# A third late tile searched by VectorE beside the attention steps, late gates from tile 21, and scores ahead of values on TensorE

## The reference, cut to what matters

```python
h = rms_norm(x, norm_g); p = h @ w_in                      # 1024 -> 2884 columns
qa, ka, va, ga, qb, kb, vb, gb, qi, ki, wi = split(p)      # ga, gb: gates of the two head groups
oa = sink_attention(window of 128 keys)                    # group A, heads 0..7
r = relu(einsum('qhe,le->qhl', qi, ki))                    # indexer
score = einsum('qhl,qh->ql', r, wi); score = where(adm, score, -inf)
_, idx = top_k(score, 256)                                 # 256 keys for each query
ob = softmax(q kT + bias over idx) v                       # group B, heads 8..15
y = x + concat(oa * silu(ga), ob * silu(gb)) @ w_out
```

## Time and profile before

| | us |
|---|---|
| median of 3 runs | 5192.75 (5189.86 to 5194.4) |
| profiled execution | 5191.41 |
| its span | 5189.6 |
| stage one, stage two, last stage in the span | 2488.8, 2103.4, 597.4 |
| busy: TensorE, its weight loads | 4365.5 (84%), 2717.3 (52%) |
| busy: VectorE, ScalarE, GpSimd | 3466.5 (67%), 3454.7 (67%), 1623.0 (31%) |

### The profile page before, as it was taken

How to read it: one execution, slowest core, us unless ns; L and a number is a source line. 1 busy time by engine, 2 the same in 40 slices (tenths; PEclk the granted TensorE clock), 3 DMA queues, 4 the chain that set the end, 5 groups by cost and what they waited for, 6 DMA issues and landing times. The chain is left out here.

```text
span 5189.6 us, 78325 instructions
## 1 busy us (share of the span) xinstructions
PE 4365.5 (84%) x26505; PEld 2717.3 (52%) x26505; DVE 3466.5 (67%) x6644; ACT 3454.7 (67%) x6887; POOL 1623.0 (31%) x1358
## 2 busy tenths in 40 slices
PE   6767777777687786767689999989999999989999
PEld 3334443434343343433466767767777776754444
DVE  1266788888797898988476766676666668625111
ACT  1578788988787797872478888858787785520100
POOL 1345556667557756777110000000000000000000
PEclk9888888888788898988799999999999999999999
DMA  6211111100010111001521111011010010034423
GB/s 143 66 44 43 37 38 39 34 30 34 30 44 32 37 45 39 33 32 56 157 64 52 43 50 39 27 53 39 25 41 25 27 37 26 12 112 134 112 102 101
DMA packets 201975, 276.98 MB, mean 53 GB/s; under 512 B 50496, under 2 KB 134176, under 8 KB 201056
## 3 DMA queue, kind: packets, MB, share of 16 engines
q1 hardware_dynamic: 198624, 271.81, 16.6%
q10 hardware_dynamic: 2960, 0.17, 0.0%
HBM read 156.73 MB, written 114.16 MB: 52 GB/s over the span
## 5 line engine op out<-in xcount | busy, mean ns | idle before, releaser
L595 PE MATMUL bank<-w,x 128*128 128x512 f32 (+1 forms) x2848 | 1245.9, 593 | 26.3 <-DVE w L940 13.7
L1042 DVE TENSOR_SCALAR_CACHE_REDUCE ties<-score,cand 128x512 int8<-128x512 f32 (+13 forms) x448 | 1110.5, 2479 | 122.3 <-POOL score L916 106.9
L595 PEld LDWEIGHTS bank<-w,x 128*128 128x128 f32 x2848 | 571.3, 204 | 608.2 <-issue 540.1
L806 ACT ACTIVATE act_junk<-score,a_cand,a_sign 128x384 int8<-128x384 f32 (+13 forms) x420 | 879.4, 2094 | 14.0
L1832 DVE CUSTOM_DVE_ANT_0 row<-bank,mask 128x512 f32<-128x512 f32 (+3 forms) x1024 | 622.5, 638 | 384.1 <-PE bank L1571 383.5
L613 PE MATMUL bank<-kiT,qi 128*128 128x512 f32 (+3 forms) x1136 | 394.2, 489 | 414.9 <-DVE kiT L960 211.4
L1538 POOL TENSOR_TENSOR near_bias<-table,mask 128x2048 f32<-128x2048 f32 (+1 forms) x32 | 129.5, 4047 | 1830.6 <-DVE part L1832 1815.1
L1766 ACT ACTIVATE pT<-bank 128x512 f32<-128x512 f32 (+2 forms) x704 | 368.0, 523 | 449.3 <-PE bank L1587 447.3
L1587 PE MATMUL bank<-ident,row 128*128 128x128 f32 x4224 | 607.3, 283 | 52.0 <-DVE pT L1943 43.4
L1668 ACT ACTIVATE row<-row,top 128x1024 f32<-128x1024 f32 (+7 forms) x640 | 632.9, 990 | 3.4 <-DVE top L1845 3.4
L1571 PE MATMUL bank<-kT,qb 64*128 64x256 f32 (+1 forms) x4352 | 608.4, 396 | 7.9 <-DVE part L1832 5.1
(11 more groups left out here) (255 smaller groups left out, 4904.9 us busy)
## 6 DMA issues: line engine op xcount, KB each, us to landing
qk_t<-ring SPq DMA_DIRECT2D x66, 256.0 KB, 2.0
gates<-ring SPq DMA_DIRECT2D x66, 256.0 KB, 2.0
gate<-gates SPq DMA_DIRECT2D x33, 512.0 KB, 3.4
out<-x_in SPq DMA_DIRECT2D x33, 512.0 KB, 2.9
x<-in_x_prompt SPq DMA_DIRECT2D x32, 512.0 KB, 3.8
mixed<-mixT SPq DMA_DIRECT2D x64, 256.0 KB, 2.0
mix_in<-mixed SPq DMA_DIRECT2D x32, 512.0 KB, 4.5
x_in<-in_x_prompt SPq DMA_DIRECT2D x32, 512.0 KB, 3.9
```

The costliest lines, as they stand in the source:

```text
L595: ins = pe.matmul(p_bank[n % 2][:, 0:n1 - n0], held[:, c * P:(c + 1) * P], w[:, c, n0:n1], start=(c == 0), stop=(c == KC - 1))
L806: tick(act.activation(junk, row, ACT.Sign, bias=c, scale=back, accum_out=a_sum[:, :]))
L1042: n = tick(dve.tensor_scalar(ties[:, 0:width], row, c.bitcast(F32), 0.0, ALU.is_ge, ALU.add, accum_out=counts[:, i:i + 1]))
```

## The change

1. `SEARCHED` goes from 30 to 29: tile 29 is no longer searched in stage one; its scores are stored like those of 30 and 31. In stage two ScalarE still searches 30 and 31 in the same tiles. VectorE searches tile 29 by itself (`test_search`), in pieces of 512 scores, with 289 portions laid evenly over the 408 wide steps of tiles 3 to 26, one portion at most between its copy and its use of scores.
2. The closing is rewritten. Tiles 30, 29 and 31 are closed in tiles 19, 27 and 29, in pieces of 512 (`close`); the mask and tie buffers hold a single piece. ScalarE stores each piece to `chosen` at the end of the step after its last portion, and VectorE's next piece waits for that store (`s_lst`). For 30 and 31 the ties are now counted beforehand by a second set of counting passes. A closing of a ScalarE tile has 34 portions, that of tile 29 has 24. SyncE loads late masks from `chosen` as it does the others. A second late row (`test_row`, 1.9 MB) is loaded at the start of stage two.
3. `LATER_FROM` goes from 23 to 21: the late gates of tiles 0 to 9 are projected in steps 21 to 30.
4. In stage two TensorE's step is transposes, scores or gate, values.

```diff
-SEARCHED = TILES - 2
+SEARCHED = TILES - 3
-LATER_FROM = 23
+LATER_FROM = 21
-LATE_SPANS = {1: ((3, 27, 28),), 2: ((3, 18, 19), (20, 28, 29))}[len(LATE_TILES)]
+ACT_TILES = LATE_TILES[1:]
+ACT_SPANS = ((3, 18, 19), (20, 28, 29))
+DVE_TILE = LATE_TILES[0]
+DVE_SPAN = (3, 26, 27)
...
+for _a, (_first, _last, _close) in zip(ACT_TILES, ACT_SPANS):
+    share(LATE_ACT, _first, _last, TESTS * (len(quarters(_a)) + 1) + 1)
+    share(LATE_DVE, _close, _close, 2 + 2 * len(quarters(_a)) + 3 * len(pieces(_a)))
+share(LATE_TEST, *DVE_SPAN[0:2], TESTS * (len(pieces(DVE_TILE)) + 1) + 1)
+share(LATE_DVE, DVE_SPAN[2], DVE_SPAN[2], 3 * len(pieces(DVE_TILE)))
...
 # load_mask
                 if t in LATE_TILES:
-                    sp.wait_ge(s_lmask, LATE_TILES.index(t) + 1)
-                    sp.dma_start(mask[t % 2][:, 0:near], late_mask[:, 0:near]).then_inc(s_m[t % 2], 16)
-                    sp.dma_start(mask[t % 2][:, near:near + NEAR], late_mask[:, near:near + NEAR]).then_inc(s_m[t % 2], 16)
-                    return
+                    sp.wait_ge(s_lst, 16 * STORED[t, len(pieces(t)) - 1])
...
 # TensorE, stage two
                     turn(n, g)
-                    if last is not None:
-                        apply(*last)
-                    last = (n, g)
                     for kind, m, j in PLACED[n, g]:
                         if kind == "score":
                             score(m, j)
                         else:
                             turn_gate(m, j)
+                    if last is not None:
+                        apply(*last)
+                    last = (n, g)
...
 # ScalarE, stage two, at the end of a step
+                    for a, q in STORES[n, g]:
+                        act.wait_ge(s_lmask, PIECE_AT[a, q] + 1)
+                        for c, m, to in stores_of(a)[q]:
+                            act.dma_start(chosen[a, :, to:to + m], late_mask[:, c:c + m]).then_inc(s_lst, 16)
...
 # VectorE, stage two
+            def close(a, held, known):
+                for q, (c, n) in enumerate(pieces(a)):
+                    at, piece, tie = held[:, c:c + n], late_mask[:, 0:n], late_tie[:, 0:n]
+                    if PIECE_AT[a, q]:
+                        dve.wait_ge(s_lst, 16 * list(STORED.values())[PIECE_AT[a, q] - 1])
+                    dve.wait_ge(s_dve, tick.n)
+                    tick(dve.tensor_scalar(piece, at, known, -BIG, ALU.is_le, ALU.mult))
+                    tick(dve.tensor_scalar(tie, at, known, None, ALU.is_equal))
+                    yield
+                    dve.wait_ge(s_dve, tick.n)
+                    tick(dve.tensor_tensor_scan(at, tie, tie, held[:, c - 1:c] if c else 0.0, ALU.add, ALU.max))
+                    yield
+                    dve.wait_ge(s_dve, tick.n)
+                    m = tick(dve.scalar_tensor_tensor(tie, at, left, tie, ALU.is_le, ALU.mult))
+                    dve.wait_ge(s_dve, m)
+                    m = tick(dve.scalar_tensor_tensor(piece, tie, BIG, piece, ALU.mult, ALU.add))
+                    dve.wait_ge(s_dve, m)
+                    dve.nop(nofuse=True).then_inc(s_lmask, 1)
+                    yield
...
+            def test_search():
+                dve.wait_ge(s_trow, 16)
+                m = tick(dve.memset(d_cand[:, 0:1], 0))
+                for i in range(TESTS):
+                    b = 31 - i
+                    c, to = d_cand[:, i % 2:i % 2 + 1], d_cand[:, (i + 1) % 2:(i + 1) % 2 + 1]
+                    for q, (c0, n) in enumerate(pieces(DVE_TILE)):
+                        dve.wait_ge(s_dve, tick.n)
+                        m = tick(dve.tensor_scalar(test_junk[:, 0:n], test_row[:, c0:c0 + n], c.bitcast(F32), 0.0, ALU.is_ge, ALU.add,
+                                                   accum_out=d_part[:, q:q + 1]))
+                        yield
+                    dve.wait_ge(s_dve, m)
+                    m = tick(dve.tensor_reduce(d_counts[:, i:i + 1], d_part[:, :], AX.X, ALU.add))
...
                     dve.tensor_copy(pT[1][at % 2][:, 0:cols], t_bank[1][:, 0:cols]).then_inc(s_c1, 1)
+                    for _ in range(LATE_TEST[n, g]):
+                        next(tests, None)
```

More of the change, by code:

```diff
@@ L1305, in quarters, with pieces, share, stores_of @@
     return [(c, min(QUARTER, (a + 1) * P - c)) for c in range(0, (a + 1) * P, QUARTER)]
+def pieces(a):
+    return [(c, min(STEP, (a + 1) * P - c)) for c in range(0, (a + 1) * P, STEP)]
 LATE_ACT = {_s: 0 for _s in STEP_AT}
 LATE_DVE = {_s: 0 for _s in STEP_AT}
[L1310 to L1316, removed]
+LATE_TEST = {_s: 0 for _s in STEP_AT}
+def share(count, first, last, many):
+    steps = wide_steps(first, last)
+    for i in range(many):
+        count[steps[i * len(steps) // many]] += 1
+for _a, (_first, _last, _close) in zip(ACT_TILES, ACT_SPANS):
[3 more added lines that the diff above has]
+share(LATE_DVE, DVE_SPAN[2], DVE_SPAN[2], 3 * len(pieces(DVE_TILE)))
+def stores_of(a):
+    far, near = ((a - 2) // 4 + 1) * STEP, (a - 1) * P
+    stores = []
+    for c, n in pieces(a):
+        parts = [(c, min(c + n, near) - c, c)] if c < near else []
+        if c + n > near:
+            at = max(c, near)
+            parts.append((at, c + n - at, far + at - near))
+        stores.append([(at - c, m, to) for at, m, to in parts])
+    return stores
+STORED, PIECE_AT = {}, {}
+for _, _a in CLOSED:
+    for _q, _parts in enumerate(stores_of(_a)):
+        PIECE_AT[_a, _q] = len(STORED)
+        STORED[_a, _q] = len(_parts) + max(STORED.values(), default=0)
+STORES = {_s: [] for _s in STEP_AT}
+for _close, _a in CLOSED:
+    _steps = wide_steps(_close, _close)
+    _front = 2 + 2 * len(quarters(_a)) if _a in ACT_TILES else 0
+    _many = _front + 3 * len(pieces(_a))
+    for _q in range(len(pieces(_a))):
+        _last = _steps[(_front + 3 * _q + 2) * len(_steps) // _many]
+        STORES[list(STEP_AT)[STEP_AT[_last] + 1]].append((_a, _q))
 def exps_of_job(n):
@@ L1415, in stage_two @@
         s_lmask = sem("late_mask_ready")
+        s_lst = sem("late_mask_stored")
+        s_trow = sem("test_row_loaded")
         s_lact = sem("late_act_ticks")
@@ L1516, in _ @@
             sp.wait_ge(s_win, 32)
+            sp.wait_ge(s_lst, 16 * max(STORED.values()))
         @block.gpsimd
@@ L1692, in late_search @@
                 act.wait_ge(s_lmade, 1)
-                for i, a in enumerate(LATE_TILES):
+                for i, a in enumerate(ACT_TILES):
                     width, parts = (a + 1) * P, quarters(a)
@@ new lines, in _ @@
+            over, left, value, low, step, more = (l_pick[:, i:i + 1] for i in range(6))
+            def close(a, held, known):
[12 more added lines that the diff above has]
+                    m = tick(dve.scalar_tensor_tensor(tie, at, left, tie, ALU.is_le, ALU.mult))
+                    dve.wait_ge(s_dve, m)
+                    m = tick(dve.scalar_tensor_tensor(piece, tie, BIG, piece, ALU.mult, ALU.add))
+                    dve.wait_ge(s_dve, m)
@@ L1927, in _ @@
+            tests = test_search()
             late_work = late_close()
```

126 lines of the change are left out of this document (70 added, 56 removed).

## The result

The changed kernel takes 5161.0 us (median of four executions, 5160.8 to 5161.1) against 5192.75: 31.8 us or 0.6% faster, the ratio 0.9939 with a 95% interval of 0.9923 to 0.9955. A fifth execution was in a slower state, 5740.5 us at a granted clock of 0.73, and is left out. Forecast were 5196 us, no change, with a range from 5163: the kernel is faster, and just outside the range. The profiled execution took 5160.8 us, its span 5159.0.

A forecast was written before the change was run, and what follows sets the result against it. No engine fills the first stage; TensorE (93% busy) bounds the attention stage. Terms -31 - 4 + 38 + 1 = +4 us on 5191.4 gave 5195.4 in the profiled execution's terms, 5196 beside the median; range 5163 to 5226.

The forecast's parts named there:

- Stage one: First stage without the search of tile 29, early gates included: -31 us, between -12 and -45.
- (b): First stage, score row 31: GpSimd's eight units take 66.4 us against 86.7 without VectorE's scans beside them, -20.3 us.
- the tail: First stage, from row 31's end to the stage's end (25.7 us): fewer late gates and stores in the way, -3.7 us.
- The +3 us for the early gates: First stage: late gates two tiles sooner delay the moment tile 28 is found by 3 us (-5 to +12).
- The closings: Attention stage, closing the three late tiles in tiles 19, 27 and 29: +27, +6 and +5, together +38 us.
- B's sign (under 100): Attention stage: tile 19 under 100 us would show that the closings are cheap.
- Rival B: Attention stage: closings cost 8 us instead of 38, as the long scan is cut into pieces; 5166 us, chance .22.
- The 9 us put down for such waits: Attention stage: VectorE's waits for mask-piece stores while closing, 4 us in tile 27 and 5 in tile 29.
- rival D: Attention stage: store waits stand open at all 21 places, 52 us instead of 16; 5232 us, chance .10.
- The tests: Attention stage, VectorE's search of tile 29 in tiles 3 to 26: 214 us of work, costing 10 us.
- Rival A: Attention stage: tests don't fit beside VectorE's bursts, 38 us instead of 10; tiles 5 to 12 each 1 us longer; 5224, chance .19.
- TensorE's order: Attention stage, scores ahead of values: 14 of 22 us of waits for VectorE's copies taken back; with the tests' 10, -4.

The follow-up runs named there:

- the last experiment: Late gate projections begun at tile 23 again, against the changed kernel with ScalarE tiles' closings spread over two tiles each: 5136.4 us, ratio 0.9891.

## Why the prediction was wrong

**Stage one was right.** Forecast -31, measured -28.8: the start of row 31 -6.1 (forecast -7.3), GpSimd -19.0 from there to the row's end (-20.3), the tail -3.7 (-3.7). What slowed GpSimd was VectorE's closing of tile 29: every multiplication is at 1.04 us now, as told; with the gates early but tile 29 in stage one (the gates alone) it is at 1.33 us and more on average, and row 31 takes 87.9 us. The attention stage began at 2460, told as near 2458. The rule of the Trainium skill on VectorE's two-input instructions (SBUF — State Buffer, Who interferes with whom) made (b) go as a whole, and so it did; the stores did not keep any of it. The +3 us for the early gates came out as a number of the trace (tile 28 found 2.8 later), but by luck. Traces with the same stage one differ by some 2 us there: 2336.9 to 2338.8 with the old one, 2338.7 to 2340.8 with the changed one. And the early gates make tile 28 sooner: by 3 to 5 us in the last experiment, and by 1.7, which is inside that spread, where they are the only change. The tail would have grown without them.

**The closings were right, for the old order.** Forecast +38, measured +35.3 with the old order. In the changed kernel they read +21.8, because the order took its share from these tiles too: 3.0, 4.5 and 6.0 us in tiles 19, 27 and 29, and without the longer closings still 3.6, 1.7 and 3.9. Tile 19 at 110.2 us with VectorE at 98.97 hits the 110 to 120 that were told as a sign, and just misses the "busy over 100"; B's sign (under 100) did not show. Rival B came nearest in time, 5166, by the wrong mechanism: it had the closings at 8 us. The three open store waits of tile 19 are where the step had them, with 5.8 us for its 7.5. The 9 us put down for such waits in tiles 27 and 29 did not come (over the stage they are 6.3 us in four places), and rival D is out.

**The tests were right in sum.** Forecast 10 us, measured 7.7 outside tile 19. Rival A is out by its price, 38. Its sign, tiles 5 to 12 each 1 us longer, does not show against the kernel before (2.7 shorter to 0.5 longer), but there the order's gain hides it. Against the kernel without tests these eight tiles are 7.1 us longer together, 4.7 of it in tiles 9 and 10, so nearly all that the tests cost lies where A looked for it. VectorE's wait for scores fell from 395.4 to 71.3 us over the stage, as told. Tile 8 is 0.5 us off, as told; tile 18 is 1.8 longer where 0.5 was allowed, at a granted clock of 0.95.

**The step that failed is TensorE's order.** "TensorE stands 68.9 us for VectorE's copies in this stage", less 21 in tiles 19 and 29 and 25 in the narrow steps: "Of the other 22 I take 14 back." Measured, alone and within the change, it gives 40: 7.5 us in tiles 19 and 29, the rest in the wide steps of the others, and nothing in the narrow steps. So taking the 25 us of the narrow steps away was right in effect, for there the wait for ScalarE's copies took the place of VectorE's. Three things were wrong. The stand was read from the matmuls' row, 68.9 us; the same wait at the weight loads is 100.2 us, and part of it shows in TensorE's busy time: alone the order took 22 us of idle time and 18 of busy time away, where the line allowed 22 in all. The 21 us of the closing tiles were taken for out of reach; but a microsecond gained ahead of a long use is passed on to the copies that follow it, in the closing tiles as well. And the wait for scores in an ordinary step (1.17 us) drew the eye: it cost nothing, since TensorE's wide step is 3.11 us in both orders. The sum with 40 in place of 14 is -22, 5169 us in the profiled execution's terms. The rest to its 5160.8 is the new work of the attention stage, which cost 37 us with the old order where closings, tests and the added load were put down at 49; stage one gave 2 less than its 31. The runs do not part this rest further.

That an order of issue could be worth more than a cap drawn from one row was not among the rivals, and should have been: the cap was the forecast's only bound there. The range missed by 2 us; with the term right the forecast would have been some 26 us lower.

## What to carry to other kernels

Read a stall of TensorE at its weight loads as well as at its matmuls, and before capping a gain by such a row, line up the steps of one undisturbed tile: the few that are longer than the rest carry the cost, and what keeps them back may lie two steps earlier. Work laid on an engine with room costs little until that engine is full in a stretch, and then its whole excess; so compare the engine's sum with the stretch's length tile by tile, and spread a block over two tiles before asking whether to move it at all (21 us for the third tile spread, nothing that could be told or a small loss unspread). Test the parts of a change singly: here one part of four brought as much as the whole.

## What the runs showed of the hardware

The granted clock of TensorE differs between kernels that issue the same matmuls. In the changed kernel tile 19, in which TensorE idles 27 of 110 us, shows 0.89, a mean of stretches at 2.4 and at 1.2 GHz, and length times one minus clock (two digits a tile) adds up to 28.7 us over the stage; with the closings spread, idle 6 of 80 us, tile 19 shows 0.96 and the sum is 12.5. The 16 us between them are an upper estimate of what the clock gave back, not a measured time. Nor does less idle time always raise the clock: the order alone took 22 us of idle time away, and the same sum stayed at 23.7 (24.2 before).

A wait of TensorE for a bank doesn't all show as its idle time. With the order alone TensorE's matmuls, the same in number and shape, were busy for 1922.1 us instead of 1940.1 at the same mean clock (0.99), while its weight loads waited 39 us less for the copies.

Beside VectorE's scan of 8.87 us GpSimd's multiplication took 8.88 us instead of 1.04; with VectorE's closing gone from that stretch all 32 of them took 1.04.

A store of 128 KB from ScalarE's queue landed 1.7 us after its issue (median of 21). The Trainium skill (DMA: Bandwidth & Descriptors, Anatomy of one DMA) gives a fixed 2.0 us for a transfer on GpSimd's path, which the prediction took for every transfer; for these stores, issued by ScalarE, the measurement is below it and decides.
